# A fused decoder layer: where the feed-forward's second weights are split, and where its third are loaded

## The chip, the cores and the metric

One NeuronCore of a Trainium2 chip runs the whole layer. The metric is the device time of one execution in microseconds (us); the number shown for a kernel is the median of its runs.

## What is computed

One layer over 256 tokens of width 1024: a mixer of three attention branches, merged by gates and projected by `w_o`, then a SwiGLU feed-forward. Both stand between RMS norms, with a modulation worked out from a condition vector. Cut to the part around the change:

```python
def rms_norm(x, g):
    return x * rsqrt(mean(x * x, axis=-1) + 1e-6) * g

y = merged @ w_o                                   # (256, 1024) @ (1024, 1024)
x = x + g1 * rms_norm(y, g_post_mix)               # the residual
h = rms_norm(x, g_pre_ffn) * (1 + sc2) + sh2       # the input of the feed-forward
gate, up = split(h @ w_up, 2)                      # w_up (1024, 2 * 2816)
y = (silu(gate) * up) @ w_down                     # w_down (2816, 1024)
x = x + g2 * rms_norm(y, g_post_ffn)
```

## The kernel before

All matrices are float32. To multiply in the faster rounded format without losing precision, each weight block is **split**: ScalarE copies the raw block into a high part (a rounded format), and VectorE subtracts it from the raw block, which leaves a low part. A product is then made of high times high, high times low, and low times high. The activations are split in the same way (`hcut` holds both parts of the feed-forward's input, `hhi` its high one).

A weight block of up to 128 x 4096 passes through one of two raw rooms, `raw[0]` and `raw[1]`, and its parts go to `whi[0]`, `wlo[0]` or `whi[1]`, `wlo[1]`. The SP queue issues nearly all loads of weights, in program order, and waits there for room. A block is split in four pieces (`q` from 0 to 3), each by one ScalarE and one VectorE instruction of 128 x 1024.

**W_o** is two blocks: its first half of the rows lies in `whi[1]`, `wlo[1]`, its second in `whi[0]`, `wlo[0]` (two pieces of its high part in `wo_early`). It is applied to the first 128 tokens (tile t = 0) and then to the second (t = 1); for each tile the first half of the rows runs over both column halves, and then the second half. So `whi[1]` and `wlo[1]` are read for the last time when the second tile is through the first half.

**The norm between** (lines 914 to 940 on ScalarE, 1282 to 1319 on VectorE) runs one tile at a time: square sums on ScalarE (line 709), the inverse root on VectorE (lines 1015 to 1027), the residual (line 1301), the second norm of the new x. TensorE transposes the new x with a diagonal matrix (`turn_x`, line 1483). Both engines then modulate a half of it each (ScalarE line 725, VectorE line 1037), and it is split (lines 734 and 1046).

**The feed-forward** has N_FFN = 11 steps of 256 gate and 256 up columns. The first step is not split: its products (`first_up`, line 1714) are taken in plain float32 from `raw[1]` itself, for tile 0 while the norm of tile 1 goes on, and for tile 1 after it. From the second step on, `up` (lines 1750 and 1751) multiplies the split weights of `whi[slot]` and `wlo[slot]` by both tiles at once: 32 pairs of matmuls, of 512 and 256 columns. `down` (lines 1398 to 1400) takes 24 matmuls a step. On TensorE they run in the order up(1), down(0), up(2), down(1), up(3) and so on, step i = 0 being the first.

Before the change the weights of step i stand in `raw[1]` for i even and in `raw[0]` for i odd, and are split to the `whi`, `wlo` of the same number. `load_step` (line 534) issues a step's two DMAs of up weights and one of down weights, on SP's queue, each behind waits:

- steps 0 and 1 (the first and the second) wait for the splits of W_o, which free the raw rooms,
- step 2 (the third) waits for `up_done` of 4: all products of the first step are made, and `raw[1]` is free,
- later steps wait until the step two before them is split.

The second step's four splits stand on ScalarE after the splits of the activations, at the head of `step(0, ...)` (line 956), and on VectorE likewise (line 1355): `whi[0]` and `wlo[0]` are free only when W_o is done (`BLOCK_DONE[B_WO + 1]`). The splits of the later steps are `cut_up_hi` (line 897, its instruction at line 905) and `cut_up_lo` (line 1304, at line 1306), two ahead of a silu and two behind it. Those of the down weights are at lines 912 and 1311. ScalarE and VectorE work in program order; a wait holds back all that stands behind it.

Of the kernel before, what the change touches and what calls it, by code (L numbers as in the profile page):

```python
# [247 lines left out]
def decoder_layer(nc, x, c, w_ada, b_ada, g_pre_mix, g_post_mix, w_in, b_gate, w_proj_sb,  # L248
                  w_proj_moba, w_proj_dsa, w_o, g_pre_ffn, g_post_ffn, w_up, w_down, out):
    ctx = ExitStack()  # L250
    with ctx:
# [216 lines left out]
        def _(sp):  # L468
# [64 lines left out]

            def load_step(i, slot, first, third=False):

                view = block_view(raw[slot], B_FFN).rearrange("p k (a n) -> p k a n", a=2)
                if first:

                    sp.wait_ge(w_hi, 4 * (B_WO + 1 + i))
                    sp.wait_ge(w_lo, 4 * (B_WO + 1 + i))  # L540
                elif third:
                    sp.wait_ge(up_done, 4)
                else:

                    sp.wait_ge(up_hi, 4 * (i - 2))
                    sp.wait_ge(up_lo, 4 * (i - 2))
                for a in range(2):
                    sp.dma_start(view[:, :, a, :], up_dram[:, :, bass.ds(i * FSTEP + FF * a, FSTEP)]).then_inc(raw_in[slot], 16)
                if first:

                    sp.wait_ge(units, BLOCK_DONE[B_WO - 1])
                    sp.wait_ge(merged, KC)
                else:
                    sp.wait_ge(d_hi, i - 1)
                    sp.wait_ge(d_lo, i - 1)
                sp.dma_start(draw[slot][:, :, :], down_dram[:, bass.ds(2 * i, 2), :]).then_inc(down_in[slot], 16)

            load_step(0, 1, True)
            load_step(1, 0, True)
            load_step(2, 1, False, True)  # L560
            with sp.Fori(3, N_FFN - 1, 2) as i:
                load_step(i, 0, False)
                load_step(i + 1, 1, False)

# [112 lines left out]
        def _(act):  # L677
# [218 lines left out]

            def cut_up_hi(i, slot, q, first=False):

                if q == 0:
                    act.wait_ge(raw_in[slot], RAW_COUNT[slot] + 16 * (i + 1 + slot))  # L900
                    if first:
                        act.wait_ge(units, BLOCK_DONE[B_WO + 1])
                    else:
                        act.wait_ge(up_done, 4 * (i - 1))
                act.activation(block_view(whi[slot], B_FFN)[:, 2 * q:2 * q + 2, :],  # L905
                               block_view(raw[slot], B_FFN)[:, 2 * q:2 * q + 2, :], ACT.Copy).then_inc(up_hi, 1)

# [6 lines left out]
            def norm_y(k, t):  # L914

                j = 2 + 2 * t if k == 0 else 6 + t
                for n in range(2):
                    if k == 0:
                        act.wait_ge(units, y_done(t, n))
                    else:  # L920
                        act.wait_ge(down_done, N_FFN - 2 + 2 * t + n + 1)
                    square_sum(j, n, bank[B_Y[k][t] + n][:, :], squares[n])
                    if k == 0 and t == 1 and n == 0:
                        modulate(0)
                root(j)

# [7 lines left out]
            norm_y(0, 0)  # L934
            norm_new_x(0)
            norm_y(0, 1)
            norm_new_x(1)
            modulate(1)
            for t in range(TT):
# [16 lines left out]
            def step(i, slot, first, last):  # L956
                if not last:
                    for q in range(4 if first else 2):
                        cut_up_hi(i + 1, 1 - slot, q, first)
                silu_tile(i, slot, 0, first)  # L960
                if not last and not first:
                    for q in range(2, 4):
                        cut_up_hi(i + 1, 1 - slot, q, first)
# [14 lines left out]
            act.wait_ge(gate_done, KC + 1)  # L978
            act.activation(whi[0][:, 0:D], gsum, ACT.Copy).then_inc(gate_hi, 1)
            step(N_FFN - 1, 1, False, True)  # L980
# [6 lines left out]
        def _(dve):  # L987
# [283 lines left out]
            for f in range(KC):  # L1271
# [7 lines left out]
                if f == 0:  # L1279
                    merge_tile(0)  # L1280

            def add_residual(k, t):

# [12 lines left out]
                if k == 0 and t == 1:  # L1296
                    modulate(0)
                inverse_root(j, lambda: gain(1))
                for n in range(2):
# [3 lines left out]

            def cut_up_lo(i, slot, q):
                dve.wait_ge(up_hi, 4 * (i - 1) + q + 1)
                dve.tensor_tensor(block_view(wlo[slot], B_FFN)[:, 2 * q:2 * q + 2, :], block_view(raw[slot], B_FFN)[:, 2 * q:2 * q + 2, :],  # L1306
                                  block_view(whi[slot], B_FFN)[:, 2 * q:2 * q + 2, :].bitcast(F32), ALU.subtract).then_inc(up_lo, 1)

# [4 lines left out]
            for t in range(TT):  # L1313
                add_residual(0, t)
                inverse_root(3 + 2 * t)
                spread_root(3 + 2 * t, t)
            modulate(TT - 1)
            for t in range(TT):
# [36 lines left out]
            def step(i, slot, last, first=False):  # L1355
                if not last:
                    for q in range(4 if first else 2):
                        cut_up_lo(i + 1, 1 - slot, q)
                if not first:
                    gate_sum(i, slot, 0)  # L1360
                f_tile(i, slot, 0, first)
                if not last and not first:
                    for q in range(2, 4):
                        cut_up_lo(i + 1, 1 - slot, q)
                f_rest(i, slot, 0)
# [16 lines left out]
            dve.wait_ge(gate_hi, 1)  # L1382
            dve.tensor_tensor(wlo[0][:, 0:D], gsum, whi[0][:, 0:D].bitcast(F32), ALU.subtract).then_inc(gate_lo, 1)
            step(N_FFN - 1, 1, True)
# [10 lines left out]
        def _(pe):  # L1395
# [331 lines left out]
            def up(i, slot, first):  # L1727
# [4 lines left out]
                for j in range(2):  # L1732
# [4 lines left out]
                    for a in range(2):  # L1737
# [37 lines left out]
            def gate_rows():  # L1775
# [6 lines left out]
                for n in range(2):  # L1782
                    cols = slice(BANK * n, BANK * (n + 1))
                    pe.matmul(bank[B_UP[0][n]][:, :], ones[:, :], whi[0][:, cols], start=True, stop=False)
                    mm = pe.matmul(bank[B_UP[0][n]][:, :], ones[:, :], wlo[0][:, cols], start=False, stop=True)
                mm.then_inc(gate_ready, 1)
# [45 lines left out]
```

## Time and profile before

| | us |
|---|---|
| median of 3 runs | 473.83 |
| lowest and highest | 473.27 and 476.32 |
| the profiled execution | 477.25 |
| its span in the trace | 475.5 |

| engine | busy, us | share of the span |
|---|---|---|
| TensorE, matmuls | 451.8 | 95% |
| TensorE, weight loads | 395.7 | 83% |
| VectorE | 325.9 | 69% |
| ScalarE | 237.7 | 50% |
| GpSimd | 61.3 | 13% |

Times in the rows are counted from the start of the span. PE is TensorE's matmul part, PEld its loading of stationary operands, DVE is VectorE, ACT ScalarE, POOL GpSimd, SPq the SP engine's queue of DMAs. Matmuls are pipelined: a busy time of one is longer than the distance from its start to the next one's, and the distance is what counts. The granted clock is a share of TensorE's full 2.4 GHz; it has two levels, 1.2 and 2.4. A wait's releaser is inferred: the engine or DMA that came last.

### The profile page before, as it was taken

What the parts mean: (1) busy time and instruction counts of PE and PEld (TensorE: products, weight loads), DVE (VectorE), ACT (ScalarE), POOL (GpSimd) and SP (SyncE); (2) the same over time, 40 slices, a digit from 0 to 9 for tenths busy, and PEclk for the clock granted to TensorE, in tenths of its full rate; (3) what the DMA queues carried; (4) which work ended last, traced back from release to release, by engine and by line L of the source; (5) the groups of instructions that cost most, each with busy time, mean ns of one, the idle gap of its engine ahead of it and who ended that gap; (6) DMA issues with size and microseconds to landing.
All of it is one profiled execution on the core that took longest, in us unless ns stands there. A gap on an engine that the chain in (4) does not pass through costs nothing.

```text
span 475.5 us, 7835 instructions
## 1 busy us (share of the span) xinstructions
PE 451.8 (95%) x2964; PEld 395.7 (83%) x2964; DVE 325.9 (69%) x562; ACT 237.7 (50%) x407; POOL 61.3 (13%) x101
## 2 busy tenths in 40 slices
PE   5899999999999899998998999899999999999994
PEld 3588989999899789988985899778888888888883
DVE  3354668786879767755994558685876696686655
ACT  4243675566766456656472348345253343534332
POOL 2000102000323111000995001000000000000000
PEclk9899999999999999999997999989999999999998
DMA  8998566878778647434779404995575657630002
GB/s 290 366 383 262 194 220 223 280 247 280 261 224 295 224 136 264 146 101 145 232 263 367 165 1 136 371 356 198 189 252 181 247 189 254 231 133 0 2 1 88
DMA packets 62658, 99.86 MB, mean 210 GB/s; under 512 B 5940, under 2 KB 42404, under 8 KB 62628
## 3 DMA queue, kind: packets, MB, share of 16 engines
q1 hardware_dynamic: 57504, 81.57, 50.7%
q0 software_dynamic: 4960, 17.84, 10.7%
q8 instruction: 19, 0.31, 0.3%
q14 instruction: 11, 0.09, 0.1%
q10 hardware_dynamic: 164, 0.05, 0.0%
HBM read 98.40 MB, written 1.05 MB: 209 GB/s over the span
## 4 chain that ended last, share of the span: by engine, by line
PE 76%; SPq 5%; DVE 5%; DMA 5%; POOL 4%; issue 2%; ACT 2%; DVEq 0%; ACTq 0%; POOLq 0%
PE psum L1750 14%; PE psum L1398 14%; PE psum L1399 13%; PE psum L1400 13%; PE psum L1751 7%; PE psum L1714 3%; SPq L480 2%; DMA raw<-in_w_in_dram 2%; DMA raw<-in_w_up_dram 2%; DVE wlo L1005 2%; SPq L488 1%; POOL xn L659 1%; PE psum L1450 1%; POOL bufp L656 1%; PE psum L1451 1%
## 5 line engine op out<-in xcount | busy, mean ns | idle before, releaser
L1750 PE MATMUL psum<-hcut,whi 128*128 128x512 f32 x320 | 114.8, 402 | 2.4 <-DVE wlo L1306 2.4
L1751 PE MATMUL psum<-hcut,wlo 128*128 128x256 f32 x320 | 90.5, 283 | 0.0
L1005 DVE TENSOR_TENSOR wlo<-raw,whi 128x768 fp32r<-128x768 f32 (+3 forms) x68 | 67.0, 1011 | 22.9 <-ACT whi L695 22.2
L1398 PE MATMUL psum<-hcut,whi 128*128 128x256 f32 x280 | 82.3, 294 | 0.3 <-DVE wlo L1005 0.3
L1399 PE MATMUL psum<-hcut,whi 128*128 128x256 f32 x280 | 79.1, 282 | 0.0
L1400 PE MATMUL psum<-hcut,wlo 128*128 128x256 f32 x280 | 79.0, 282 | 0.0
L1750 PEld LDWEIGHTS psum<-hcut,whi 128*128 128x128 f32 x320 | 60.9, 190 | 17.7 <-issue 2.8
L1751 PEld LDWEIGHTS psum<-hcut,wlo 128*128 128x128 f32 x320 | 61.1, 191 | 0.4
L695 ACT ACTIVATE whi<-raw 128x768 fp32r<-128x768 f32 (+3 forms) x68 | 55.7, 850 | 6.7 <-PE psum L1671 4.7
L1398 PEld LDWEIGHTS psum<-hcut,whi 128*128 128x128 f32 x280 | 53.4, 191 | 5.5 <-ACT qk L767 2.3
L1399 PEld LDWEIGHTS psum<-hcut,whi 128*128 128x128 f32 x280 | 53.5, 191 | 0.0
L1400 PEld LDWEIGHTS psum<-hcut,wlo 128*128 128x128 f32 x280 | 53.4, 191 | 0.0
L1306 DVE TENSOR_TENSOR wlo<-raw,whi 128x1024 fp32r<-128x1024 f32 x40 | 47.1, 1220 | 7.0 <-ACT whi L905 7.0
L1311 DVE TENSOR_TENSOR dlo<-draw,dhi 128x2048 fp32r<-128x2048 f32 x11 | 25.1, 2292 | 37.6 <-ACT dhi L912 37.6
L905 ACT ACTIVATE whi<-raw 128x1024 fp32r<-128x1024 f32 x40 | 39.8, 1046 | 5.7 <-DMA raw<-in_w_up_dram 5.7
L950 ACT ACTIVATE fsil<-fsil 128x256 f32<-128x256 f32 x20 | 8.4, 418 | 61.8 <-DVE fsil L1323 61.8
L1399 PE MATMUL psum<-dlo,fhi 128*128 128x512 f32 x88 | 34.4, 391 | 0.0
L1398 PE MATMUL psum<-dhi,fhi 128*128 128x512 f32 x88 | 34.3, 390 | 0.0
L1400 PE MATMUL psum<-dhi,flo 128*128 128x512 f32 x88 | 34.3, 390 | 0.0
L912 ACT ACTIVATE dhi<-draw 128x2048 fp32r<-128x2048 f32 x11 | 20.9, 1913 | 24.6 <-PE psum L1400 24.6
L600 POOL DMA_DIRECT2D xn<-in_w_ada_dram x24 | 13.0, 540 | 144.1 <-DVE acc L1078 70.6
L1399 PE MATMUL psum<-wlo,hcut 128*128 128x320 f32 (+2 forms) x80 | 28.9, 361 | 0.0
(229 smaller groups left out, 882.2 us busy)
## 6 DMA issues: line engine op xcount, KB each, us to landing
raw<-in_w_up_dram SPq DMA_DIRECT2D x22, 1024.0 KB, 7.5
xn<-in_w_ada_dram POOLq DMA_DIRECT2D x32, 512.0 KB, 5.1
raw<-in_w_in_dram SPq DMA_DIRECT2D x6, 2048.0 KB, 8.9
draw<-in_w_down_dram SPq DMA_DIRECT2D x11, 1024.0 KB, 4.9
ada<-in_w_ada_dram SPq DMA_DIRECT2D x16, 512.0 KB, 9.4
raw<-in_w_in_dram SPq DMA_DIRECT2D x3, 1536.0 KB, 8.8
raw<-in_w_o_dram SPq DMA_DIRECT2D x8, 512.0 KB, 6.0
raw<-in_w_in_dram SPq DMA_DIRECT2D x3, 1280.0 KB, 7.0
```

The lines of the kernel that those rows point to most:

```text
L695: act.activation(block_view(whi[b % 2], b)[0:p, chunks, cols], block_view(raw[b % 2], b)[0:p, chunks, cols], ACT.Copy).then_inc(w_hi, 1)
L905: act.activation(block_view(whi[slot], B_FFN)[:, 2 * q:2 * q + 2, :], block_view(raw[slot], B_FFN)[:, 2 * q:2 * q + 2, :], ACT.Copy).then_ ...
L912: act.activation(dhi[slot][:, :, :], draw[slot][:, :, :], ACT.Copy).then_inc(d_hi, 1)
L1005: dve.tensor_tensor(block_view(wlo[b % 2], b)[0:p, chunks, cols], block_view(raw[b % 2], b)[0:p, chunks, cols], block_view(whi[b % 2], b)[ ...
L1306: dve.tensor_tensor(block_view(wlo[slot], B_FFN)[:, 2 * q:2 * q + 2, :], block_view(raw[slot], B_FFN)[:, 2 * q:2 * q + 2, :], block_view(w ...
L1311: dve.tensor_tensor(dlo[slot][:, :, :], draw[slot][:, :, :], dhi[slot][:, :, :].bitcast(F32), ALU.subtract).then_inc(d_lo, 1)
L1398: pe.matmul(dst, a[0], b[0], start=first, stop=False)
L1399: pe.matmul(dst, a[0], b[1], start=False, stop=False)
L1400: return pe.matmul(dst, a[1], b[0], start=False, stop=last)
L1714: mm = pe.matmul(bank[j][:, S * a + P * t:S * a + P * (t + 1)], w[:, k, FSTEP * a + P * j:FSTEP * a + P * (j + 1)], hx[:, t, k, :], start= ...
L1750: pe.matmul(dst[:, :], wh, hcut[:, k, :, :].rearrange("p a s -> p (a s)"), start=k == 0, stop=False)
L1751: mm = pe.matmul(dst[:, S:2 * S], wl, hhi[:, k, :], start=False, stop=k == KC - 1)
```

## The change

The raw rooms and the rooms of the split parts no longer go together.

- The **second step's** up weights still land in `raw[0]`, but are split to `whi[1]` and `wlo[1]`, where the first half of W_o was. The wait is for `BLOCK_DONE[B_WO]`, the second tile's end with that half. The four pieces stand between the steps of the norm: the first after the first tile's norm of the new x; the second amid the second tile's square sums, behind the first tile's modulation; the third and fourth after the second tile's norm of the new x, ahead of its modulation.
- The **third step's** up weights are loaded into `raw[0]`, as soon as the second step's are split, and no longer into `raw[1]` behind the first step's products. They are split to `whi[0]`, `wlo[0]`.
- From there on every step changes its room: an even step is in `raw[0]`, an odd one in `raw[1]`. The wait for `up_done` of 4 stands ahead of the fourth step's load into `raw[1]`. Rooms and order of the down weights stay the same.
- The gate's row near the end, which used `whi[0]`, `wlo[0]`, uses `whi[1]`, `wlo[1]`.

```diff
 SP's queue
-            load_step(0, 1, True)
-            load_step(1, 0, True)
-            load_step(2, 1, False, True)
+            for i in range(2):
+                sp.wait_ge(w_hi, 4 * (B_WO + 1 + i))
+                sp.wait_ge(w_lo, 4 * (B_WO + 1 + i))
+                load_up(i, 1 - i)
+                if i == 0:
+
+                    sp.wait_ge(units, BLOCK_DONE[B_WO - 1])
+                    sp.wait_ge(merged, KC)
+                load_down(i, 1 - i)
...
+            sp.wait_ge(up_hi, 4)
+            sp.wait_ge(up_lo, 4)
+            load_up(2, 0)
+            sp.wait_ge(d_hi, 1)
+            sp.wait_ge(d_lo, 1)
+            load_down(2, 1)
+            sp.wait_ge(up_done, 4)
             with sp.Fori(3, N_FFN - 1, 2) as i:
-                load_step(i, 0, False)
-                load_step(i + 1, 1, False)
+                load_step(i, 1)
+                load_step(i + 1, 0)
 ScalarE
+            def second_up_hi(q):
 
                 if q == 0:
+                    act.wait_ge(raw_in[0], RAW_COUNT[0] + 32)
+                    act.wait_ge(units, BLOCK_DONE[B_WO])
+                act.activation(block_view(whi[1], B_FFN)[:, 2 * q:2 * q + 2, :],
+                               block_view(raw[0], B_FFN)[:, 2 * q:2 * q + 2, :], ACT.Copy).then_inc(up_hi, 1)
...
                     if k == 0 and t == 1 and n == 0:
                         modulate(0)
+                        second_up_hi(1)
...
             norm_y(0, 0)
             norm_new_x(0)
+            second_up_hi(0)
             norm_y(0, 1)
             norm_new_x(1)
+            second_up_hi(2)
+            second_up_hi(3)
             modulate(1)
...
-                if not last:
-                    for q in range(4 if first else 2):
-                        cut_up_hi(i + 1, 1 - slot, q, first)
+                if not last and not first:
+                    for q in range(2):
+                        cut_up_hi(i + 1, slot, q)
 VectorE
+            def second_up_lo(q):
+
+                dve.wait_ge(up_hi, q + 1)
+                dve.tensor_tensor(block_view(wlo[1], B_FFN)[:, 2 * q:2 * q + 2, :], block_view(raw[0], B_FFN)[:, 2 * q:2 * q + 2, :],
+                                  block_view(whi[1], B_FFN)[:, 2 * q:2 * q + 2, :].bitcast(F32), ALU.subtract).then_inc(up_lo, 1)
...
                 if k == 0 and t == 1:
                     modulate(0)
+                    second_up_lo(1)
...
                 spread_root(3 + 2 * t, t)
+                for q in ((0,), (2, 3))[t]:
+                    second_up_lo(q)
             modulate(TT - 1)
...
-                if not last:
-                    for q in range(4 if first else 2):
-                        cut_up_lo(i + 1, 1 - slot, q)
+                if not last and not first:
+                    for q in range(2):
+                        cut_up_lo(i + 1, slot, q)
 TensorE, in up
-                            wh, wl = [block_view(x[slot], B_FFN)[:, k, FSTEP * a + P * j:FSTEP * a + P * (j + 1)] for x in (whi, wlo)]
+                            wh, wl = [block_view(x[1 - slot], B_FFN)[:, k, FSTEP * a + P * j:FSTEP * a + P * (j + 1)] for x in (whi, wlo)]
```

## Rows read from the trace of the kernel before

**Rows 1.** Busy time by stretch: start:end, length, engines, clock, DMA share, GB/s.

```profile
270.00:280.00 10.00, 10.00 (x79) 9.50 (x78) 5.91 (x19) 4.34 (x14) 0.00 (x0) 1.00 0.01 2
...
300.00:310.00 10.00, 7.76 (x38) 6.21 (x36) 6.44 (x8) 4.63 (x6) 0.00 (x0) 1.00 1.07 371
310.00:320.00 10.00, 9.85 (x47) 8.61 (x48) 8.73 (x11) 4.56 (x6) 0.53 (x1) 0.83 1.02 350
...
360.00:380.00 20.00, 20.00 (x105) 17.03 (x104) 12.03 (x14) 8.13 (x10) 0.53 (x1) 1.00 0.71 243
```

**Rows 2.** What TensorE waited for, 100 to 475 us: total, times, longest.

```profile
PE psum L1750 <- DVE wlo L1306: 2.4, 1, 2.4
PE psum L1398 <- POOL hcut L650: 2.2, 1, 2.2
...
PE psum L1714 <- ACT xn L725: 0.7, 1, 0.7
```

**Rows 3.** The chain that ended last, around the gap: start, length, what.

```profile
291.66 10.29 DMA raw<-in_w_up_dram
...
308.69 1.23 DVE wlo L1306
```

**Rows 4.** Timeline, SP's queue: start, length, what; third and fourth steps' up weights.

```profile
291.24 0.99 SPq L548 DMA_DIRECT2D raw<-in_w_up_dram  x2
...
297.49 2.65 SPq L548 DMA_DIRECT2D raw<-in_w_up_dram  x2
```

**Rows 5.** Timeline, TensorE around the gap; brackets hold idle before and its releaser.

```profile
290.96 0.47 PE L1750 MATMUL psum<-hcut,whi 128*128 128x512 f32 x1
...
302.15 0.40 PE L1398 MATMUL psum<-dhi,fhi 128*128 128x512 f32 x1
...
307.37 0.39 PE L1400 MATMUL psum<-dhi,flo 128*128 128x512 f32 x1
310.15 0.49 PE L1750 MATMUL psum<-hcut,whi 128*128 128x512 f32 x1 [2.39 <-DVE wlo L1306]
...
314.24 0.41 PE L1750 MATMUL psum<-hcut,whi 128*128 128x512 f32 x1
```

**Rows 6.** Timeline, TensorE: second tile's first matmul with W_o's second half.

```profile
266.70 0.40 PE L1398 MATMUL psum<-wo_early,hcut 128*128 128x512 f32 x1
```

**Rows 7.** DMA issues, 254 to 268 us: second step's up weights; last is us to landing.

```profile
raw<-in_w_up_dram SPq DMA_DIRECT2D x2, 1024.0 KB, 10.4
```

**Rows 8.** Timeline, ScalarE, in the norm and at the splits.

```profile
269.66 0.60 ACT L709 ACTIVATE fsil<-psum 128x512 f32<-128x512 f32 x1 [3.11 <-PE psum L1400]
...
274.20 0.60 ACT L709 ACTIVATE fsil<-psum 128x512 f32<-128x512 f32 x1 [2.14 <-PE psum L1400]
...
282.24 1.51 ACT L725 ACTIVATE xn<-psum,col 128x128 f32<-128x128 f32 x4 [2.95 <-PE psum L1483]
...
285.70 3.89 ACT L905 ACTIVATE whi<-raw 128x1024 fp32r<-128x1024 f32 x4
...
302.06 2.01 ACT L905 ACTIVATE whi<-raw 128x1024 fp32r<-128x1024 f32 x2 [5.65 <-DMA raw<-in_w_up_dram]
```

**Rows 9.** Timeline, VectorE, in the norm and at the third step's splits.

```profile
270.38 0.69 DVE L1290 TENSOR_TENSOR xn<-psum,gb 128x512 f32<-128x512 f32 x1 [2.57 <-ACT fsil L709]
...
275.00 0.16 DVE L1021 SCALAR_TENSOR_TENSOR var<-ssq,var 128x1 f32<-128x1 f32 x1 [2.12 <-ACT fsil L709]
...
283.13 1.36 DVE L1037 TENSOR_SCALAR xn<-psum,col 128x128 f32<-128x128 f32 x4 [2.58 <-PE psum L1483]
...
303.15 2.36 DVE L1306 TENSOR_TENSOR wlo<-raw,whi 128x1024 fp32r<-128x1024 f32 x2 [3.98 <-ACT whi L905]
```

**Rows 10.** Groups of VectorE's instructions, 236 to 256 us, GpSimd working: busy, mean ns.

```profile
L1012 DVE TENSOR_TENSOR wlo<-raw,whi 128x1024 fp32r<-128x1024 f32 x6 | 9.6, 1645 | 0.0
```

**Rows 11.** Timeline, TensorE: the matmuls with W_o behind the 2.2 us gap.

```profile
253.10 0.76 PE L1398 MATMUL psum<-wo_early,hcut 128*128 128x512 f32 x1 [2.25 <-POOL hcut L650]
...
259.87 0.39 PE L1398 MATMUL psum<-whi,hcut 128*128 128x512 f32 x1
```

More of the change, by code:

```diff
@@ L532, in _, with load_up @@
                 load(b)
[L534 to L546, printed above, removed]
-                for a in range(2):
-                    sp.dma_start(view[:, :, a, :], up_dram[:, :, bass.ds(i * FSTEP + FF * a, FSTEP)]).then_inc(raw_in[slot], 16)
-                if first:
+            def load_up(i, part):
+                view = block_view(raw[part], B_FFN).rearrange("p k (a n) -> p k a n", a=2)
+                for a in range(2):
+                    sp.dma_start(view[:, :, a, :], up_dram[:, :, bass.ds(i * FSTEP + FF * a, FSTEP)]).then_inc(raw_in[part], 16)
@@ L551, in load_step, with load_down @@
+            def load_down(i, slot):
+                sp.dma_start(draw[slot][:, :, :], down_dram[:, bass.ds(2 * i, 2), :]).then_inc(down_in[slot], 16)
+            for i in range(2):
[3 more added lines that the diff above has]
+                if i == 0:
                     sp.wait_ge(units, BLOCK_DONE[B_WO - 1])
                     sp.wait_ge(merged, KC)
-                else:
-                    sp.wait_ge(d_hi, i - 1)
-                    sp.wait_ge(d_lo, i - 1)
@@ L556, in load_step @@
-                sp.dma_start(draw[slot][:, :, :], down_dram[:, bass.ds(2 * i, 2), :]).then_inc(down_in[slot], 16)
-            load_step(0, 1, True)
-            load_step(1, 0, True)
-            load_step(2, 1, False, True)
+                load_down(i, 1 - i)
+            def load_step(i, part):
+                sp.wait_ge(up_hi, 4 * (i - 2))
+                sp.wait_ge(up_lo, 4 * (i - 2))
+                load_up(i, part)
+                sp.wait_ge(d_hi, i - 1)
+                sp.wait_ge(d_lo, i - 1)
+                load_down(i, 1 - part)
@@ L895, in _, with cut_up_hi @@
             load_roots()
-            def cut_up_hi(i, slot, q, first=False):
+            def second_up_hi(q):
                 if q == 0:
[L900 to L906, printed above, removed]
+                    act.wait_ge(raw_in[0], RAW_COUNT[0] + 32)
+                    act.wait_ge(units, BLOCK_DONE[B_WO])
+                act.activation(block_view(whi[1], B_FFN)[:, 2 * q:2 * q + 2, :],
+                               block_view(raw[0], B_FFN)[:, 2 * q:2 * q + 2, :], ACT.Copy).then_inc(up_hi, 1)
+            def cut_up_hi(i, part, q):
+                if q == 0:
+                    act.wait_ge(raw_in[part], RAW_COUNT[part] + 16 * (i + 2 - part))
+                    act.wait_ge(up_done, 4 * (i - 1))
+                act.activation(block_view(whi[part], B_FFN)[:, 2 * q:2 * q + 2, :],
+                               block_view(raw[part], B_FFN)[:, 2 * q:2 * q + 2, :], ACT.Copy).then_inc(up_hi, 1)
             def cut_down_hi(i, slot, first=False):
@@ L962, in step @@
                     for q in range(2, 4):
-                        cut_up_hi(i + 1, 1 - slot, q, first)
+                        cut_up_hi(i + 1, slot, q)
                 f_part(i, slot, 0)
@@ L978, in _ @@
             act.wait_ge(gate_done, KC + 1)
-            act.activation(whi[0][:, 0:D], gsum, ACT.Copy).then_inc(gate_hi, 1)
+            act.activation(whi[1][:, 0:D], gsum, ACT.Copy).then_inc(gate_hi, 1)
             step(N_FFN - 1, 1, False, True)
@@ L1302, in add_residual, with cut_up_lo @@
                                              ALU.mult, ALU.add).then_inc(x_new, 1)
-            def cut_up_lo(i, slot, q):
+            def cut_up_lo(i, part, q):
                 dve.wait_ge(up_hi, 4 * (i - 1) + q + 1)
-                dve.tensor_tensor(block_view(wlo[slot], B_FFN)[:, 2 * q:2 * q + 2, :], block_view(raw[slot], B_FFN)[:, 2 * q:2 * q + 2, :],
-                                  block_view(whi[slot], B_FFN)[:, 2 * q:2 * q + 2, :].bitcast(F32), ALU.subtract).then_inc(up_lo, 1)
+                dve.tensor_tensor(block_view(wlo[part], B_FFN)[:, 2 * q:2 * q + 2, :], block_view(raw[part], B_FFN)[:, 2 * q:2 * q + 2, :],
+                                  block_view(whi[part], B_FFN)[:, 2 * q:2 * q + 2, :].bitcast(F32), ALU.subtract).then_inc(up_lo, 1)
             def cut_down_lo(i, slot):
@@ L1363, in step @@
                     for q in range(2, 4):
-                        cut_up_lo(i + 1, 1 - slot, q)
+                        cut_up_lo(i + 1, slot, q)
                 f_rest(i, slot, 0)
@@ L1382, in _ @@
             dve.wait_ge(gate_hi, 1)
-            dve.tensor_tensor(wlo[0][:, 0:D], gsum, whi[0][:, 0:D].bitcast(F32), ALU.subtract).then_inc(gate_lo, 1)
+            dve.tensor_tensor(wlo[1][:, 0:D], gsum, whi[1][:, 0:D].bitcast(F32), ALU.subtract).then_inc(gate_lo, 1)
             step(N_FFN - 1, 1, True)
@@ L1783, in gate_rows @@
                     cols = slice(BANK * n, BANK * (n + 1))
-                    pe.matmul(bank[B_UP[0][n]][:, :], ones[:, :], whi[0][:, cols], start=True, stop=False)
-                    mm = pe.matmul(bank[B_UP[0][n]][:, :], ones[:, :], wlo[0][:, cols], start=False, stop=True)
+                    pe.matmul(bank[B_UP[0][n]][:, :], ones[:, :], whi[1][:, cols], start=True, stop=False)
+                    mm = pe.matmul(bank[B_UP[0][n]][:, :], ones[:, :], wlo[1][:, cols], start=False, stop=True)
                 mm.then_inc(gate_ready, 1)
```

## The prediction

> **What bounds the kernel.** I read the profile in this order. The table of stages first: from 314 us on TensorE never rests (20.00 of 20.00 us in a stretch in the middle of the feed-forward), while 300 to 310 us has only 7.76 of 10.00 us and the stretch behind it a granted clock of 0.83 [rows 1]. So the end of the kernel is set by TensorE, and what can be won lies where it idles. The list of what TensorE waited for has three gaps from 240 us on: 2.2 us ahead of W_o, 0.7 us ahead of the second token tile's first products, and 2.4 us at line 1750, released by a low-part split on VectorE [rows 2]. The chain says what stands behind the last one: the load of the third step's up weights, 10.29 us from 291.66, then the splits on ScalarE and VectorE, to 308.69 + 1.23 = 309.92 [rows 3]. That load starts when it does because its room, raw[1], is freed by the last of the first step's products, at 291.24 [rows 4].
>
> **The price of that gap.** TensorE, row by row [rows 5]: the second step's 32 pairs of matmuls start at 290.96, the first step's down products at 302.15, a pair is (302.15 - 290.96) / 32 = 0.350. The last of 24 down products starts at 307.37; with their pitch of (307.37 - 302.15) / 23 = 0.227 the third step could start at 307.60. It starts at 310.15: **2.55 us** idle. Behind it the clock falls to 1.2 GHz for a while: the seven pairs from 310.15 to 314.24 take 4.09 us where full speed needs 7 x 0.350 = 2.45: **1.64 us**. Together 4.19 us.
>
> **Part 1: the second step's splits move.** Out of ScalarE's four splits from 285.70 (3.89 us) and VectorE's four behind them, into gaps of the norm, written to whi[1] and wlo[1], free as soon as the second token tile has been through the first half of W_o: its last such matmul is issued before 266.70, so about 266.9 [rows 6]. The weights were asked for from 254 us and took 10.4 us, so they are there at about 264.9 [rows 7]. A split costs ScalarE 3.89 / 4 = 0.97 us in a row and 1.04 alone; VectorE 1.23, two of them 2.36 [rows 3, 8, 9]. The gaps:
> - First split. ScalarE idles 3.11 us before 269.66, so from 266.55: split 266.9 to 268.0, 1.6 left. VectorE idles 2.57 before 270.38: 268.0 to 269.2, 1.1 left.
> - Second. ScalarE idles 2.14 before 274.20, from 272.06: done at 273.1. VectorE idles 2.12 before 275.00: 273.2 to 274.4, with one small operation of 0.14 pushed behind it to 274.6; 0.4 left.
> - Third and fourth. ScalarE idles 2.95 before 282.24, from 279.29: done at 281.3, 0.9 left. VectorE idles 2.58 before 283.13, from 280.55: 280.6 + 2.36 = 283.0. Only about 0.15 us is left before its half of the modulation, and TensorE's fifth matmul after 283.80 wants that half.
>
> These three gaps hide all eight operations, so I price the move at nothing. Below nothing it can't be: nothing on TensorE's path waited for the second step's splits (in the list of its waits they show only once, for the third step's). The other end: VectorE's same split beside a working GpSimd took 1.645 us on average [rows 10]; two are 3.29, ending at 283.84, 0.7 us too late. GpSimd does nothing in this stretch [rows 1], so I take the 1.23. The Trainium skill (SBUF — State Buffer, Who interferes with whom) says the same from the ports: a VectorE instruction with two SBUF inputs contends with GpSimd instructions that read SBUF. It is the rule that speaks against moving such splits, and by it the sum would lose 0.7 us only if GpSimd worked here.
>
> **Part 2: the third step's load.** It now goes to raw[0] and waits for the fourth low split, at 283.0, not for 291.24: 8.2 us earlier. With the duration that it has now (10.7 us from issue to landing, shared with others) it lands at 293.7; it will have the DMA engines nearly alone and be quicker. Issued on SP's queue: two DMAs as before, and behind them the down weights, which wait for VectorE's first down split as before. The new wait on up_done stands behind these and is met by then; the fourth step's load, now into raw[1], is issued when the first down split is done, at about 296 (now 297.49 [rows 4]).
>
> **Part 3: what the splits of the third step then wait for.** Not the load: ScalarE is free at 302.06 - 5.65 = 296.41, VectorE at 303.15 - 3.98 = 299.17, both at the latest, as the eight splits no longer stand ahead of their work of the first step [rows 8, 9]. The pattern from VectorE's start of the first such split to the end of the fourth, with the sums and the silu between, took 309.92 - 303.15 = 6.77 us. From 299.17 that ends at 305.9, and some 0.8 us sooner if the first step's work closes up. TensorE wants it at 307.60: 1.7 us or more to spare, so the gap is gone whole, and with it the fall of the clock. Late next would be the fourth step's weights. Draw(2), raw(3) and draw(3) are 4.2 MB from about 297.5; at 371 GB/s [rows 1] that is 11.3 us, to 308.8. ScalarE asks at about 310 (its down split waits for the down products' end, then takes 1.9), its splits and VectorE's are over by 320, and TensorE wants them at 307.60 + 32 x 0.350 + 24 x 0.227 = 324.2. So it waits for nothing.
>
> **Sum.** 0 - 2.55 - 1.64 = -4.2 us. The profiled execution took 477.25 (span 475.5 and 1.75 around it) and would take 473.0. The median of the runs is 473.83, 3.4 below the profiled one; nothing in the sum depends on what makes up those 3.4, so it goes to **469.6**, 0.9% less.
>
> **Rivals.**
> A. *The clock's share is another.* Low clock behind a gap is not one price: ahead of W_o, after 2.2 us of idle, the 15 matmuls from 253.10 to 259.87 took 6.77 us instead of 15 x 0.227 = 3.41, so 3.36 lost [rows 2, 11]; here it was 1.64. For: same kind of gap. If the executions without profile lose nothing there, the gain is 2.55 and the time 471.3; if they lose 3.36, it is 5.9 and 467.9. The Trainium skill (TensorE: Matmul & The Clock Gate, Part 1) says that the number of slow matmuls varies from run to run, 6 to 14 at the start of one kernel; as an estimate from that page, at 0.29 / 2 a matmul, 0.9 to 2.0 us here.
> B. *The splits in the norm make it slower.* Place: VectorE ahead of 283.13. If the third and fourth low splits stand wholly in front of the modulation, the gap of 0.71 before 283.80 grows by 2.36 to 3.1 us, and the clock falls behind it. Price 2.36 + 3.36 = 5.7 against 4.2 won: 475.3. It decides from an idle of about 2.2 us, the shortest that had a fall behind it. Against: I find 0.15 us in hand and at worst 0.7 late, giving 1.4.
> C. *The third step stalls all the same*, since the load is not what ends last: VectorE is late by its own queue. Each us beyond the 1.7 in hand gives one us back. If the splits end at 309.92 as now nothing is won: 473.8. Against: ScalarE sat 5.65 us waiting for that DMA alone.
>
> **Chances.** Forecast 0.62 (its own range 468.8 to 470.6, by half the spread of the clock's price and 0.5 of lateness); A 0.22, half above, half below; C 0.08; B 0.05; the rest 0.03. The range 468.0 to 471.8 leaves out B, C and the ends of A. A measurement of this kernel can tell about 1% from no change: 469.1 or less is faster. That is the lower third of the forecast and A's half below: 0.62 x 0.33 + 0.11 = 0.32. Slower (from 478.6) would need more than B gives: 0.02. Within 1%: 0.66.
>
> **What would show it.** In the profile after: TensorE has no wait at line 1750 for a low split and no clock below 1.00 between 300 and 320; the third step's two DMAs issue near 283 and the span is 471.3. Two high and two low splits stand between 279.3 and 283.0. Part 1 is wrong if the 0.71 before the second tile's products has grown; part 3 if a wait for VectorE or a DMA is left before the third or fourth step; A if the idle is gone but the time fell by 2.5 or 6.

## The result

The changed kernel took 472.3 us (median of 12 runs, 470.9 to 473.1), the kernel before 475.5 us over the 12 runs beside it. One of these took 633.2 us and is left out of the ratio; the other 11 have a mean of 475.4. The ratio of the means is 0.993, with a 95% interval of 0.991 to 0.995: faster by 0.7%, within the 1% that counts as the same. The forecast was 469.6 in a range of 468.0 to 471.8, so the time lies above the range. The changed kernel's profiled execution took 472.39 (span 470.7), against 473.0 (span 471.3) forecast for it.

So the profiled execution came out 0.6 us lower than forecast and the median 2.7 us higher. Both have to be explained. Two numbers say where to look for the second: the median that I started from, 473.83 of three runs, was low (81 runs of the kernel before, in the later comparisons, have a mean of 475.5), and the gain was 3.3 us and not 4.2.

### The profile page after: what moved, and what is told of

Read it like the earlier page. It is cut to its first block, busy times and chain, and to the rows that moved or that the text cites. A ratio compares the mean times of both kernels' runs of the same rounds, so it can differ in the third digit from the quotient of the medians.

```text
span 470.7 us, 7835 instructions
## 1 busy us (share of the span) xinstructions
PE 447.8 (95%) x2964; PEld 392.2 (83%) x2964; DVE 326.1 (69%) x562; ACT 238.1 (51%) x407; POOL 61.2 (13%) x101
## 3 DMA queue, kind: packets, MB, share of 16 engines
HBM read 98.40 MB, written 1.05 MB: 211 GB/s over the span
## 4 chain that ended last, share of the span: by engine, by line
PE 79%; SPq 5%; POOL 4%; DVE 4%; DMA 2%; issue 2%; ACT 2%; DVEq 0%; POOLq 0%; ACTq 0%
PE psum L1778 16%; PE psum L1426 14%; PE psum L1427 13%; PE psum L1428 13%; PE psum L1779 8%; PE psum L1742 3%; SPq L480 2%; DMA raw<-in_w_in_dram 2%; DVE wlo L1024 2%; SPq L488 2%; POOL xn L669 1%; POOL hcut L660 1%; PE psum L1478 1%; POOL bufp L666 1%; PE psum L1479 1%
## 5 line engine op out<-in xcount | busy, mean ns | idle before, releaser
L1778 PE MATMUL psum<-hcut,whi 128*128 128x512 f32 x320 | 113.4, 398 | 0.0
L1332 DVE TENSOR_TENSOR wlo<-raw,whi 128x1024 fp32r<-128x1024 f32 x36 | 42.4, 1220 | 3.0 <-ACT whi L920 3.0
L920 ACT ACTIVATE whi<-raw 128x1024 fp32r<-128x1024 f32 x36 | 35.9, 1045 | 0.0
```

The lines of the kernel that those rows point to most:

```text
L920: act.activation(block_view(whi[part], B_FFN)[:, 2 * q:2 * q + 2, :], block_view(raw[part], B_FFN)[:, 2 * q:2 * q + 2, :], ACT.Copy).then_ ...
L1332: dve.tensor_tensor(block_view(wlo[part], B_FFN)[:, 2 * q:2 * q + 2, :], block_view(raw[part], B_FFN)[:, 2 * q:2 * q + 2, :], block_view(w ...
```

## The profile after

The same stretches as in [rows 1], from the table of stages of the changed kernel (length, then PE, PEld, DVE, ACT, POOL busy, granted clock, DMA share, GB/s):

```profile
270.00:280.00 10.00, 10.00 (x79) 9.50 (x79) 7.46 (x23) 6.19 (x15) 0.00 (x0) 1.00 0.01 2
...
300.00:310.00 10.00, 10.00 (x52) 8.41 (x51) 6.64 (x10) 5.99 (x8) 0.00 (x0) 1.00 1.08 368
310.00:320.00 10.00, 10.00 (x57) 8.58 (x56) 9.59 (x12) 3.79 (x6) 0.53 (x1) 1.00 0.83 292
360.00:380.00 20.00, 20.00 (x109) 17.10 (x108) 15.25 (x18) 8.67 (x11) 0.53 (x1) 1.00 0.61 198
```

TensorE works through 300 to 320 us, at full clock. VectorE and ScalarE do more between 270 and 280, where the second step's splits now are. What TensorE waited for, 100 to 470 us, against [rows 2]:

```profile
PE psum L1426 <- POOL hcut L660: 3.0, 2, 2.3
...
PE psum L1742 <- ACT xn L735: 0.7, 1, 0.7
```

The wait for a low split is gone, and the 0.7 before the second tile's first products has not grown. (The 3.0 amid W_o are two waits here, of 2.3 and 0.7.) (Lines have moved: 1426 is 1398, 1742 is 1714, 1778 is 1750.) SP's queue, against [rows 4]: the third step's weights are asked for at 282.03, not 291.24, and the fourth's at 295.77, not 297.49.

```profile
282.03 0.99 SPq L538 DMA_DIRECT2D raw<-in_w_up_dram  x2
294.97 0.37 SPq L542 DMA_DIRECT2D draw<-in_w_down_dram  x1
295.77 1.02 SPq L538 DMA_DIRECT2D raw<-in_w_up_dram  x2
```

TensorE at the start of the third step, against [rows 5]: the last down product and the first up product are 0.23 apart, and the pairs come 0.35 apart at once.

```profile
306.56 0.40 PE L1428 MATMUL psum<-dhi,flo 128*128 128x512 f32 x1
306.79 0.39 PE L1778 MATMUL psum<-hcut,whi 128*128 128x512 f32 x1
...
307.14 0.40 PE L1778 MATMUL psum<-hcut,whi 128*128 128x512 f32 x1
```

ScalarE's splits and their surroundings, against [rows 8]: one amid the norm's two tiles, one behind the first tile's modulation, two ahead of the second's, with 1.55, 1.20 and 1.05 us of idle left behind them.

```profile
266.18 1.06 ACT L912 ACTIVATE whi<-raw 128x1024 fp32r<-128x1024 f32 x1 [0.50 <-DMA raw<-in_w_up_dram]
268.80 0.60 ACT L719 ACTIVATE fsil<-psum 128x512 f32<-128x512 f32 x1 [1.55 <-PE psum L1428]
...
271.07 1.07 ACT L912 ACTIVATE whi<-raw 128x1024 fp32r<-128x1024 f32 x1
273.34 0.60 ACT L719 ACTIVATE fsil<-psum 128x512 f32<-128x512 f32 x1 [1.20 <-PE psum L1428]
...
278.33 1.99 ACT L912 ACTIVATE whi<-raw 128x1024 fp32r<-128x1024 f32 x2
281.38 1.50 ACT L735 ACTIVATE xn<-psum,col 128x128 f32<-128x128 f32 x4 [1.05 <-PE psum L1511]
```

VectorE, against [rows 9]: its two last splits end at 281.95, and 0.31 us of idle is left before its half of the modulation.

```profile
279.60 2.35 DVE L1304 TENSOR_TENSOR wlo<-raw,whi 128x1024 fp32r<-128x1024 f32 x2
282.27 1.36 DVE L1056 TENSOR_SCALAR xn<-psum,col 128x128 f32<-128x128 f32 x4 [0.31 <-PE psum L1511]
...
297.35 2.35 DVE L1332 TENSOR_TENSOR wlo<-raw,whi 128x1024 fp32r<-128x1024 f32 x2
...
301.74 2.36 DVE L1332 TENSOR_TENSOR wlo<-raw,whi 128x1024 fp32r<-128x1024 f32 x2 [0.38 <-ACT whi L920]
```

The third step's low splits end at 304.1, TensorE wants them at 306.79: 2.7 us in hand.

## The experiments

Each was timed beside the kernel before on the same chip. The comparisons of this section together have 81 runs of the kernel before; the changed kernel has 31, with the 12 of the result. Every run comes with its granted clock, the mean over its span, and that turned out to matter. I compare mean times, with twice the standard error behind them, where small differences count.

### The changed kernel again, and its runs

Two more sets of the changed kernel. The first:

> The changed kernel again, timed on one chip beside the kernel before. If the prediction's terms hold in every execution (2.55 us of idle and 1.64 us of low clock both gone), it is 4.2 us below the kernel before, a ratio of 0.991. If the clock's share was larger in the one profiled execution than it is on average, the gain is between 2.55 and 4.2 us, a ratio of 0.9912 to 0.9946, and it differs from run to run with the granted clock. If something in the norm costs time, the gain is under 2.5 us and the gap of 0.70 us before the second tile's first products has grown.

It gave 472.3 us (7 runs), ratio 0.992 (0.989 to 0.996). The second:

> The changed kernel once more, for the average of its gain over more runs and for the comparison with the reordered one on the same chip. Over the two sets of runs so far its mean span is 470.4 us against 473.85 of the kernel before, 3.4 less. If the clock's share of the third step's gap is a matter of chance from run to run (0 in some, 1.5 in the profiled ones), this set lies at 2.8 to 4.2 too; if it is fixed, at 4.2.

It gave 472.3 (12 runs), ratio 0.993 (0.991 to 0.996). Together with the first 12: a mean of 472.2 +- 0.4, against 475.5 +- 0.4 before. The gain is 3.3 +- 0.5 us.

What the runs look like is more telling than their mean:

| | lowest | highest | runs at a clock of 0.998 or more: mean |
|---|---|---|---|
| before | 473.0 | 479.1 | 473.8 (10 of 81 runs) |
| changed | 470.7 | 474.0 | 471.0 (6 of 31 runs) |

The kernel before has 39 of its 81 runs below 475.3 and 33 from 476 to 478, with 3 between 475.5 and 476: two humps. The runs whose clock hardly fell are 2.8 us apart, near the 2.55 of the idle alone. If every run of the kernel before has the idle, the clock's share is about 3.3 - 2.8 = 0.5 us on average, or 3.3 - 2.55 = 0.8 if the idle of the one trace is taken for all; the profiled execution had 1.64. Either is no surer than the 3.3, that is within some 0.5; but 1.64 is out of it. The granted clock of a whole run is only a rough sign: it counts falls that cost nothing too. The profiled execution of the kernel before had one between 20 and 50 us (0.94), and W_o began at 244.54 all the same, as in the traces of the changed kernel.

The three traces of the changed kernel show where its own spread comes from. "Products" are the first step's, for the first tile:

| trace | W_o's first matmul, us | first products, us | span, us | W_o to products | products to the end |
|---|---|---|---|---|---|
| before | 244.54 | 274.00 | 475.5 | 29.5 | 201.5 |
| changed | 244.34 | 273.14 | 470.7 | 28.8 | 197.6 |
| second set | 244.64 | 274.52 | 472.2 | 29.9 | 197.7 |
| third set | 244.34 | 274.66 | 472.1 | 30.3 | 197.4 |

What the change touches is the last column, 3.8 to 4.1 us less than before. The rest of the difference between spans arises amid W_o, where the clock falls for a longer or a shorter stretch. That looks like chance: the kernels below that leave W_o as it is took 28.2 to 30.0 us for the same stretch. By the other two traces of the changed kernel the spans differ by 3.3 and 3.4 us, not 4.8.

### The load put back

```diff
             sp.wait_ge(up_hi, 4)
             sp.wait_ge(up_lo, 4)
+            sp.wait_ge(up_done, 4)
             load_up(2, 0)
...
-            sp.wait_ge(up_done, 4)
```

> The second step's splits stay in the norm, but the third step's load waits again for the first step's products (up_done of 4). Theory one (the load is what ended last): all of the gain goes, the time is that of the kernel before within 0.5 us, TensorE waits some 2.4 us for the low splits before the third step, and ScalarE waits for the DMA. Theory two (the splits behind the norm kept ScalarE and VectorE busy, and that was the cause): the gain stays for the most part, 2 us or more below the kernel before.

476.6 us, ratio 1.001 (0.998 to 1.004): all of the gain is gone, with the splits still in the norm. (The mean is 0.6 +- 1.0 above that of the kernel before.) The list of waits of this kernel, 285 to 312 us:

```profile
ACT whi L920 <- PE psum L1779: 6.9, 1, 6.9
DVE wlo L1332 <- ACT whi L920: 5.6, 2, 5.2
...
PE psum L1778 <- DVE wlo L1332: 2.7, 1, 2.7
```

ScalarE stands idle for 6.9 us until the third step's weights are there. The list names TensorE as the releaser; the chain of this kernel, which follows the end back, names the load instead:

```profile
290.88 10.58 DMA raw<-in_w_up_dram
```

TensorE then waits 2.7. In the timeline the clock falls right behind it: pairs 0.64 apart, not 0.35.

```profile
309.67 0.79 PE L1778 MATMUL psum<-hcut,whi 128*128 128x512 f32 x1 [2.68 <-DVE wlo L1332]
310.25 0.41 PE L1779 MATMUL psum<-hcut,wlo 128*128 128x256 f32 x1
310.46 0.63 PE L1778 MATMUL psum<-hcut,whi 128*128 128x512 f32 x1
310.89 0.41 PE L1779 MATMUL psum<-hcut,wlo 128*128 128x256 f32 x1
311.10 0.63 PE L1778 MATMUL psum<-hcut,whi 128*128 128x512 f32 x1
```

Theory one holds: the early load is the whole gain. The moved splits bring nothing by themselves; they make the room for it.

### The load half as late

```diff
             sp.wait_ge(up_lo, 4)
+            sp.wait_ge(up_done, 2)
             load_up(2, 0)
```

> The third step's load waits for the first half of the first step's products for tile 1 (up_done of 2), so it is issued near 286.5 instead of 282.0, 4.5 us later. If the load has the slack that its early landing says (it landed before ScalarE asked at 294.6), the time is that of the changed kernel within 0.5 us. If the landing sets the start of the third step, 2 us or more of the gain are gone.

472.4 us, ratio 0.993 (0.990 to 0.996), as the changed kernel. Of the 9.2 us by which the change makes the load earlier, some 3.4 were enough. In this kernel's trace the load is issued at 287.89 (286.5 was expected, and it was at 291.24 before) and ScalarE waits 0.55 us for it at 296.25, at no cost:

```profile
296.25 2.01 ACT L921 ACTIVATE whi<-raw 128x1024 fp32r<-128x1024 f32 x2 [0.55 <-DMA raw<-in_w_up_dram]
```

### The idle kept, the clock held up

```diff
             down(0, 1, True)
+            pe.wait_ge(gate_summed, 1)
+            warm_up(20)
             with pe.Fori(...)
```

on top of the kernel with the late load.

> As the kernel with the late load, and 20 small transposes of the identity stand on TensorE in the idle before the third step (about 20 x 0.112 = 2.2 us, in a bank that is free by then); they do nothing for the output. They hide no wait, they only keep TensorE at work. The difference to the kernel with the late load is the price of the low clock: 1.6 us if it is the same in all executions as in the profiled one, up to 3.4 us by the gap ahead of W_o, 0 if the clock does not matter here or falls all the same.

In its profiled execution this works as meant: the transposes take 2.3 us of the idle, 0.46 are left, and the pairs behind come 0.35 apart at once. That execution has a span of 472.8, the profiled one with the late load alone 475.0; 1.5 of these 2.2 us lie behind the start of the third step (309.00 and 309.67), the others had come by then. The median is 476.0, ratio 1.001 (0.999 to 1.004). Over all runs the difference is much less: mean spans of 473.8 +- 0.6 and 474.4 +- 0.9. (The span, since this kernel spends some 0.4 us more around it than the others.) The difference of 0.6 has an uncertainty of 1.1, so this kernel alone doesn't settle the clock's share: it is in line with 0.5, and 1.6 is just within its reach.

### The other gap that is filled

Both kernels with the same transposes in the 2.2 us of idle amid W_o:

```diff
                         if t == 0 and n == 0:
+                            if kk == 1:
+                                pe.wait_ge(gated, 3 * KC)
+                                warm_up(20)
                             pe.wait_ge(w_hi, 4 * (B_WO + 1) + kk + 1)
```

> The kernel before with 20 small transposes of the identity (2.2 us, no use for the output) in TensorE's 2.2 us idle amid W_o. Over the runs so far the spans of the kernel before lie between 471.4 and 477.3 us, with a granted clock of 0.985 to 0.999; the theory is that two gaps share this spread, the one amid W_o and the one ahead of the third step. If so the filled kernel is some 1 to 2 us faster on average and no longer reaches its slowest values, but still varies by the third step's gap. If the transposes only lengthen the path, it is slower by up to 0.5 us with the same spread.

> The changed kernel with the same 20 transposes amid W_o. It has no idle over 0.8 us left behind the start, so by the theory its clock stays near 0.998 in all runs, its spread shrinks to under 1 us, and its mean span is near 469.2, that of the changed kernel's runs at clock 0.998. Its distance to the kernel before so filled is the third step's gap alone: 2.55 us of idle and the clock's average share, 0.6 by the averages so far, 1.6 by the one profile. If the spread comes from elsewhere it stays at 2 us or more.

The kernel before so filled: 475.1 us, ratio 0.999 (0.996 to 1.001), mean 475.3 +- 0.8, from 473.4 to 477.9. The changed one: 471.8, ratio 0.994 (0.991 to 0.997), mean 472.2 +- 1.0, from 470.3 to 474.6. Both expectations failed: no clear gain, and the spread stays. (These two kernels spend 0.3 and 0.4 us more around the span than the others. In mean spans they are 0.5 +- 0.7 and 0.4 +- 1.0 us below the kernels without transposes, which is no clear gain either. And the changed one does have an idle left that its expectation denies, of 1.7 us near 162 us.) In the profiled executions the clock stays up amid W_o, and the stretch from W_o's first matmul to the first step's first products takes 27.6 and 27.3 us, where it took 29.5 in the kernel before and 28.8 to 30.3 in the changed one. (The profiled run of the changed one, 470.3 us, was the fastest of its 8.) So the fall behind that gap is real in a profiled execution, but the transposes are in no way free in the others, or the spread is not made there alone. Which, I can't tell from these runs. The distance between the two filled kernels, 3.1 +- 1.3 us, agrees with 3.3.

### One and two splits too many in the norm

The rival on the slower side, priced. Ahead of the third and fourth low splits:

```diff
+                if t == 1:
+                    dve.wait_ge(units, BLOCK_DONE[B_WO + 1])
+                    for q in range(2):        # or range(1)
+                        then(dve.tensor_tensor(block_view(wlo[0], B_FFN)[:, 2 * q:2 * q + 2, :], ...))
                 for q in ((0,), (2, 3))[t]:
                     second_up_lo(q)
```

> The changed kernel with two more low splits on VectorE (to room not in use, no use for the output) ahead of the third and fourth, in the norm of the second tile. Each takes about 1.2 us, and 0.3 us are in hand there by the changed kernel's trace. The rival that the splits in the norm cost time, priced: TensorE's products of the second tile come about 2.1 us later, and if an idle of that length brings the clock down, 1.6 us more; 2.1 to 3.8 us above the changed kernel. If VectorE's modulation is not on the path there, nothing changes.

> One more low split on VectorE in the second tile's norm, where two cost 3.7 us of mean span (2.1 of it the lateness, the rest the clock). With 0.3 us in hand and 1.25 for the split, TensorE's products of the second tile pause about 1.0 us behind their fourth matmul. If so short an idle leaves the clock up, it costs 1.0 us; if the clock falls as behind the longer ones, 2.5.

Two: 476.1 us, ratio 1.002 (0.999 to 1.004), mean 3.7 +- 0.9 us above the changed kernel: the whole gain, and a little. One: 473.4, ratio 0.996 (0.993 to 0.998), mean 1.4 +- 0.7 above. TensorE's timelines, first of the kernel with two,

```profile
282.82 1.16 PE L1747 MATMUL psum<-xn,raw 128*128 128x128 f32 x8 [0.70 <-ACT xn L735]
285.70 8.14 PE L1747 MATMUL psum<-xn,raw 128*128 128x128 f32 x56 [1.72 <-DVE xn L1056]
```

then of the kernel with one:

```profile
283.81 1.16 PE L1747 MATMUL psum<-xn,raw 128*128 128x128 f32 x8 [0.71 <-ACT xn L735]
285.42 6.52 PE L1747 MATMUL psum<-xn,raw 128*128 128x128 f32 x56 [0.45 <-DVE xn L1056]
```

It is not the fifth matmul that waits for VectorE's half but the ninth. With two extra splits it waits 1.72 us, and the 56 matmuls behind take 8.14 us instead of 6.52: the clock fell, for 1.6 us. With one it waits 0.45 and the clock stays. Both traces give the same reserve: 1.23 - 0.45 and 2.46 - 1.72 are 0.8 and 0.7 us, more than the 0.31 of idle that I counted in the expectations, since the ninth matmul comes later than the fifth. So the third and fourth splits stand where some 0.8 us are in hand, and one more would have cost 1.4 us, two the whole gain.

### Another order in W_o

The gap amid W_o filled with work that has to be done: both tiles go through the first half of W_o before either goes through the second.

```diff
             for t in range(TT):
                 if t == 1:
                     pe.wait_ge(gated, 3 * KC)
...
                     for n in range(2):
                         mm = out_part(t, 0, n, kk)
                 mm.then_inc(units, 1)
+            for t in range(TT):
                 for n in range(2):
```

> The changed kernel with TensorE's order in W_o changed: both tiles go through the first half of W_o's rows before either goes through the second half. The second tile's 24 matmuls (5.5 us) then fill the idle amid W_o with work that has to be done anyhow. The first tile's result comes at about the same time as now, 5.5 us of products less a gap of 3.0 and a low clock of 1.4 to 3.4; the second tile's comes about 6.8 us earlier. If TensorE is then bound by the norms' chains, its products for the first step's second tile start 3 us or so earlier than at 282.9, and the time falls to about 468; if the norm of the second tile waits for the modulation of the first, under 1 us is won.

473.8 us, ratio 0.995 (0.992 to 0.997), 1.1 +- 0.7 above the changed kernel in the mean, where a fall to 468 was expected. The place of the first tile's transpose was wrong now. It stood between the second tile's column halves and waited for the norm, with the rest of W_o queued behind it, and the clock fell (TensorE's timeline of this kernel):

```profile
267.66 3.78 PE L1511 MATMUL psum<-xn,xt 128*128 128x128 f32 x16 [3.69 <-DVE xn L1050]
271.09 0.77 PE L1426 MATMUL psum<-wo_early,hcut 128*128 128x512 f32 x1
271.66 0.63 PE L1427 MATMUL psum<-wlo,hcut 128*128 128x512 f32 x1
```

So the transpose was moved behind both halves, and the second step's splits with it: the second beside the third ahead of the modulation, the fourth behind the splits of the activations (ScalarE's edit is shown, VectorE's is alike).

```diff
-                    if t == 1 and n == 0:
-                        turn_x(0)
+                if t == 1:
+                    turn_x(0)
...
-                        second_up_hi(1)
...
-            second_up_hi(2)
-            second_up_hi(3)
+            second_up_hi(1)
+            second_up_hi(2)
             modulate(1)
             for t in range(TT):
                 cut_h(t)
+            second_up_hi(3)
```

> W_o in the new order again, and now the transpose of the first tile stands behind both column halves of the second tile (it stalled TensorE for 3.7 us between them). The second step's splits: the first where it was, the second and third ahead of the second tile's modulation, the fourth behind the splits of the activations, where the half-late load showed 4.5 us of room. Expected: the transpose waits about 1.3 us, the first tile's products run from 270.3 to 277.6, the second tile's start near 280.4 instead of 282.9; 2 to 3 us below the changed kernel, median near 469.5. If the norm's chain for the second tile is held up by the first tile's modulation, under 1 us.

469.6 us, ratio to the kernel before 0.987 (0.984 to 0.991), mean 2.6 +- 0.4 us below the changed kernel. This one beats both. Its 6 runs lie between 469.4 and 470.0, where the changed kernel's 31 spread over 3.3 us: in its trace no idle of TensorE over 0.93 us is left behind 200 us, and its clock was 0.996 or more in every run. TensorE, in the norm:

```profile
267.38 2.05 PE L1511 MATMUL psum<-xn,xt 128*128 128x128 f32 x16 [0.93 <-DVE xn L1050]
270.23 7.38 PE L1743 MATMUL psum<-xn,raw 128*128 128x128 f32 x64 [0.79 <-ACT xn L735]
277.45 1.95 PE L1511 MATMUL psum<-xn,xt 128*128 128x128 f32 x16
280.10 2.16 PE L1743 MATMUL psum<-xn,raw 128*128 128x128 f32 x17 [0.70 <-ACT xn L735]
```

The second tile's products start at 280.10, where 280.4 was expected.

## Why the prediction was right and where it was wrong

**What bounds the kernel, and the cause of the gap: right.** With the load late again the wait of 2.7 us and the whole time came back; with it half late nothing did.

**Part 1, the splits in the norm at no cost: right.** The 0.7 before 283.80 is 0.70 now [rows 2]. The smallest reserve was put at 0.15 us; the idle left there is 0.31, and the two kernels with extra splits put the whole reserve at some 0.8. Two details were off. The second step's weights landed at about 266.1, not 264.9 [rows 7]: the 10.4 us was a median of two DMAs, and the split needs the later one. ScalarE waited 0.50 us for them, within its reserve. And TensorE wants VectorE's half at the ninth matmul, not the fifth, so there was more room than counted. The rule of the Trainium skill (SBUF — State Buffer, Who interferes with whom) on a VectorE instruction with two SBUF inputs beside GpSimd's reads had nothing to act on. GpSimd was at rest (0.00 us busy from 270 to 280), and the splits took 1.23 us alone and 2.35 for two, not the 1.645 of [rows 10].

**Parts 2 and 3: right.** The load went out at 282.03 in the profile, the splits had ended 2.7 us before TensorE wanted them where 1.7 or more was forecast, and no later step waited.

**The sum in the profiled execution: right for the change's part, with some luck in the total.** 4.2 us were forecast and the profiled spans differ by 4.8. Of that, 3.4 us (310.15 to 306.79) had come by the start of the third step, 0.9 of them from W_o and no work of the change (283.80 against 282.93 for the second tile's products); the rest is the low clock behind it. So the change's part is 3.9, a little under the forecast, and the total would have been 3.3 or 3.4 with either of the other two traces of the changed kernel.

**The step that failed is the one from the profile to the median.** I wrote that nothing in the sum depends on what makes up the 3.4 us between the profiled execution and the median. It does, in two ways.

First, the base. 473.83 is the median of three runs, and the mean of the 81 later ones is 475.5: 1.7 of the 2.7 us that were missing. From 475.5 the same 4.2 us would have led to 471.3, inside the range. The time has two humps, and two of these three runs lie in the lower one. Their clocks are not on record; of the 81, those between 473.5 and 474.2 have 0.992 to 0.999, those from 476 on 0.981 to 0.994.

Second, the clock's term. I took 1.64 us, read from one execution of 477.25 us with the low clock of 0.981, whole off a median of other runs. The term is mis-sized: on average it is 0.5 to 0.8 us, within some 0.5, which is the other 1 us or so. Why it is less is not shown. All three traces with this gap (before, the load put back, the kernel before with W_o filled) have a fall behind it, of 1.6 us each by the count of the prediction. No trace shows an execution in which the clock stayed up there; that there are such runs is what the averages suggest. (475.5 - 2.55 - 0.5 = 472.4, near the 472.2 measured, is no test of it, as the 0.5 comes out of the same runs.)

**Rival A** had named the second (the clock's share is another) and put its lower end at 471.3, 2.55 below the same base of 473.83. The measured gain of 3.3 lies between its lower end and the forecast; the measured time lies above both, because of the base. The Trainium skill (TensorE: Matmul & The Clock Gate, Part 1) says that the number of slow matmuls at a kernel's start differs from run to run. The traces agree for the gap amid W_o: behind it the matmuls run at half the clock until about 258 us in one trace of the changed kernel and until 260.5 in another. But the 0.9 to 2.0 us that I estimated from that page for the third step's gap lie above the average that the runs show.

**Rival B** was priced at 5.7 us at most, for splits wholly in front of the modulation. Two splits too many cost 3.7 +- 0.9; in the trace 1.7 of it is waiting and 1.6 the clock. The mechanism is real, and it was some 0.8 us away. **Rival C** did not come: no wait for a split or a DMA is left before the third or the fourth step.

**Chances.** Within 1% had the most, 0.66, and came. The forecast's own range, 468.8 to 470.6 at 0.62, did not. The range was too narrow at its upper end, as it took account of an uncertain gain but not of an uncertain base.

## What to carry to other kernels

When a load ends a chain, ask what holds its room, and whether work that stands elsewhere can free it sooner; then the moved work needs only a gap, and the reserve of the tightest gap is what decides. What the clock's fall behind a gap costs in one profiled execution is not its average: take the idle off the median, and the fall only by its average over many runs. And take the median itself from more than three runs, when a time has two humps. And before a gap is filled with waste work, look for work that has to be done anyhow: the same gap gave nothing that can be told from noise for the transposes, and 2.6 us for the reordered products, once the transpose stood where it waits for little.

## What was not expected of the hardware

The same program on the same data differs by 6 us from run to run (473.0 to 479.1 in 81 runs), in two humps, with the granted clock between 0.981 and 0.999. The kernel whose idles from 200 us on are 0.93 us or less varies by 0.6 us (6 runs). In the traces part of the spread is made amid W_o: from its first matmul to the first products the changed kernel took 28.8, 29.9 and 30.3 us, and from there to the end 197.4 to 197.7.

The length of one idle does not say whether the clock falls. In the profiled executions it stayed behind one of 1.7 us near 162 us, in which all these kernels wait for VectorE, and fell behind one of 1.72 in the norm, which had one of 0.70 just ahead of it. Amid W_o it fell right behind the idle of 2.25 in the kernel before, but in the changed kernel's trace only behind a second, shorter idle:

```profile
252.98 0.48 PE L1426 MATMUL psum<-wo_early,hcut 128*128 128x512 f32 x1 [2.28 <-POOL hcut L660]
253.29 0.39 PE L1427 MATMUL psum<-wlo,hcut 128*128 128x512 f32 x1
...
254.64 0.76 PE L1426 MATMUL psum<-whi,hcut 128*128 128x512 f32 x1 [0.73 <-POOL hcut L660]
255.20 0.63 PE L1427 MATMUL psum<-wlo,hcut 128*128 128x512 f32 x1
```

What exactly makes the two humps is open: filling the gap amid W_o with transposes did not remove them.
